# Scores of two heads issued together on the two halves of TensorE's rows, in two attentions of a two-block kernel

## The chip, the cores and the metric

The kernel runs on one core of a Trainium2 chip. The metric is the device time of one execution in microseconds; the median of three runs is given.

## What is computed

Two transformer blocks over 256 rows of width 1024, in float32. Only the parts with the two attentions that the change touches matter here:

```python
# first block: attention over keys chosen by an index score, 8 heads of 64
s = einsum(q, k) * 64 ** -0.5 - slopes[head] * distance     # masked keys -inf
out = softmax(s) @ v
# beside it: a causal depthwise convolution of 31 taps over 512 channels
# second block: banded attention, 8 heads of 64, with a relative bias per head
sc = einsum(qb, kb) * 64 ** -0.5 + rel_bias[head, clip(distance)]
ob = softmax(sc) @ vb
# and differential attention, 4 heads with two components of 64 each
attn = softmax(q0 k0) - lam * softmax(q1 k1);  oa = attn @ va
```

The second block goes on with a gated merge, a cross attention over 256 memory rows and a feed-forward layer.

## The kernel before

All engines run programs written out by hand, ordered by semaphores; there is no scheduler. Weights come as blocks of 1 MB on SP's queue. ScalarE rounds each half block (a "piece" of 1024 columns) to `w_hi` (L1232), VectorE makes the rest `w_lo` (L1696), in a ring of four slots, and TensorE multiplies a piece in 12 matmuls of 512 columns (L564 to L566). Ten pieces of the first block are "native": eight matmuls (L597) on unsplit weights, and neither ScalarE nor VectorE works for them.

`attention` on TensorE serves the first attention (tag `a1_`) and the banded one (`b_`). `STEPS` (L365) lists 16 steps (h, t): head h, row block t of 128 rows, with 128 keys for t = 0 and 256 for t = 1. Step n on TensorE is: transposes of the probabilities (`turn_p`, L804, one for t = 0 and two for t = 1, into bank 6), the scores of step n + 2 (L795) into bank 4 or 5, one piece of a projection for later (`between`), and the values of step n - 1 (L811, two records for t = 0, four for t = 1). A score has 64 rows, one head's width: even heads lie on rows 0 to 63, odd ones on 64 to 127. Each matmul of float32 scores or values leaves two records in the trace.

For step n VectorE adds the bias tile `bias_t` to the scores and takes the reduction in the same instruction (L2035 in the first attention, L1846 in the banded one); ScalarE takes the exponential (L1320), rounds a piece's weights, and copies the turned probabilities to `pT` (L1406). In the first attention the bias tile is made for every step (L2013) and VectorE also works off the convolution's taps (L1914), up to nine a step (`A1_TAPS`). In the banded one the tile is made once for each head (L1840). Scores of steps 0 and 1 are issued ahead of the loop, behind them one piece, and ahead of that VectorE and ScalarE already do their part of these steps (`project_slabs`).

In the banded attention TensorE also transposes the rotated keys of the differential attention, behind the piece of steps 1 and 2 (`TURN_AT`), four at a time into bank 7 (L1072), and ScalarE copies them to `kaT` (L1290). Behind the banded attention the differential one starts: its `d_scores` (L1088) issues the scores of a head's two components one behind the other, on the two row halves, into banks 4, 5 and 7 in turn (`D_BANKS`); its transposes are at L1098, its values at L1105.

## Time and profile before

| | |
|---|---|
| median of 3 runs | 954.34 us (953.24 to 954.71) |
| span of the profiled execution | 953.0 us |
| TensorE busy | 918.4 us, 96% of the span |
| VectorE busy | 627.9 us, 66% |
| ScalarE busy | 458.5 us, 48% |
| first attention | about 126 to 199 us |
| banded attention | about 519 to 586 us |

The time of the profiled execution itself is not listed apart from its span, which is 1.3 us below the median of the runs: that is what lies around a span. Ends of matmuls are modelled, so the distance between starts says more than a duration. A share of busy time is a mean over stages with different limits.

### The profile page before, as it was taken

What the parts mean: (1) busy time and instruction counts of PE and PEld (TensorE: products, weight loads), DVE (VectorE), ACT (ScalarE), POOL (GpSimd) and SP (SyncE); (2) the same over time, 40 slices, a digit from 0 to 9 for tenths busy, and PEclk for the clock granted to TensorE, in tenths of its full rate; (3) what the DMA queues carried; (4) which work ended last, traced back from release to release, by engine and by line L of the source; (5) the groups of instructions that cost most, each with busy time, mean ns of one, the idle gap of its engine ahead of it and who ended that gap; (6) DMA issues with size and microseconds to landing.
All of it is one profiled execution on the core that took longest, in us unless ns stands there. A gap on an engine that the chain in (4) does not pass through costs nothing.

```text
span 953.0 us, 11982 instructions
## 1 busy us (share of the span) xinstructions
PE 918.4 (96%) x4235; PEld 735.6 (77%) x4235; DVE 627.9 (66%) x1022; ACT 458.5 (48%) x709; POOL 31.7 (3%) x42
## 2 busy tenths in 40 slices
PE   4999999999999999999999999999999999999997
PEld 3877755688788888887887777788888788888785
DVE  4898999988755555676748445678656565555444
ACT  0554523465544444443654554674545465555442
POOL 2110000010000000000000000000000000000000
PEclk9999999999999999999999999999999999999999
DMA  9999324656485565575555343455451475655531
GB/s 331 353 386 352 114 79 145 232 204 219 134 265 180 190 192 187 195 263 171 189 190 184 91 152 112 133 177 199 149 204 46 133 221 183 190 193 182 177 133 44
DMA packets 103030, 178.10 MB, mean 187 GB/s; under 512 B 6318, under 2 KB 52635, under 8 KB 102986
## 3 DMA queue, kind: packets, MB, share of 16 engines
q1 hardware_dynamic: 96138, 151.23, 48.2%
q0 software_dynamic: 6848, 26.28, 7.5%
q8 instruction: 27, 0.44, 0.2%
q14 instruction: 17, 0.14, 0.0%
HBM read 176.39 MB, written 1.05 MB: 186 GB/s over the span
## 4 chain that ended last, share of the span: by engine, by line
PE 74%; DVE 12%; issue 7%; DMA 3%; ACT 2%; SPq 0%; POOL 0%; DVEq 0%; POOLq 0%; ACTq 0%
PE bank L564 18%; PE bank L566 18%; PE bank L565 18%; PE bank L976 10%; DVE conv_out L1914 5%; DVE w_lo L1696 2%; DMA tap_rows<-in_w_dw 1%; DMA raw_weights<-in_w_in 1%; ACT w_hi L1232 1%; PE bank L955 1%; DVE ada_acc L1772 1%; PE bank L643 1%; DMA ada_raw<-in_w_ada 1%; PE bank L795 1%; PE bank L635 1%
## 5 line engine op out<-in xcount | busy, mean ns | idle before, releaser
L1696 DVE TENSOR_TENSOR w_lo<-raw_weights,w_hi 128x1024 fp32r<-128x1024 f32 x267 | 324.2, 1223 | 229.2 <-ACT w_hi L1232 227.8
L1232 ACT ACTIVATE w_hi<-raw_weights 128x1024 fp32r<-128x1024 f32 x267 | 281.0, 1059 | 282.1 <-PE bank L566 200.3
L564 PE MATMUL bank<-w_hi,a_hi 128*128 128x512 f32 x808 | 323.5, 400 | 3.1 <-issue 1.3
L566 PE MATMUL bank<-w_hi,a_lo 128*128 128x512 f32 x808 | 315.9, 391 | 0.0
L565 PE MATMUL bank<-w_lo,a_hi 128*128 128x512 f32 x808 | 315.6, 391 | 0.0
L564 PEld LDWEIGHTS bank<-w_hi,a_hi 128*128 128x128 f32 x808 | 152.1, 188 | 40.6 <-issue 8.5
L566 PEld LDWEIGHTS bank<-w_hi,a_lo 128*128 128x128 f32 x808 | 152.1, 188 | 32.7
L565 PEld LDWEIGHTS bank<-w_lo,a_hi 128*128 128x128 f32 x808 | 152.4, 189 | 29.7 <-issue 0.2
L976 PE MATMUL bank<-w_hi,ff_hi 128*128 128x512 f32 x176 | 55.1, 394 | 0.8 <-DVE hidden_rows L2194 0.5
L976 PE MATMUL bank<-w_lo,ff_hi 128*128 128x512 f32 x176 | 54.2, 389 | 0.0
L976 PE MATMUL bank<-w_hi,ff_lo 128*128 128x512 f32 x176 | 54.2, 389 | 0.0
L1914 DVE SCALAR_TENSOR_TENSOR conv_out<-conv_in,conv_taps_T,conv_out 128x256 f32<-128x256 f32 x120 | 51.4, 489 | 0.0
L1320 ACT ACTIVATE probabilities<-masked_scores,row_stats 128x128 f32<-128x128 f32 (+1 forms) x32 | 14.6, 455 | 58.6 <-DVE row_stats L2035 41.4
L976 PEld LDWEIGHTS bank<-w_hi,ff_hi 128*128 128x128 f32 x176 | 32.7, 188 | 8.6 <-DVE hidden_rows L2194 0.9
L976 PEld LDWEIGHTS bank<-w_hi,ff_lo 128*128 128x128 f32 x176 | 33.0, 188 | 6.9
L976 PEld LDWEIGHTS bank<-w_lo,ff_hi 128*128 128x128 f32 x176 | 33.0, 188 | 6.9
L597 PE MATMUL bank<-raw_weights,feature_rows_early 128*128 128x512 f32 x80 | 36.7, 604 | 0.0
L597 PEld LDWEIGHTS bank<-raw_weights,feature_rows_early 128*128 128x128 f32 x80 | 14.5, 189 | 17.0 <-issue 16.5
L1772 DVE SCALAR_TENSOR_TENSOR ada_acc<-ada_start,row_stats,ada_acc 128x512 f32<-128x512 f32 x35 | 26.3, 751 | 1.1
L564 PE MATMUL bank<-w_hi,mem_hi 128*128 128x512 f32 x64 | 25.9, 404 | 0.0
L566 PE MATMUL bank<-w_hi,mem_lo 128*128 128x512 f32 x64 | 25.0, 391 | 0.0
L565 PE MATMUL bank<-w_lo,mem_hi 128*128 128x512 f32 x64 | 25.0, 390 | 0.0
(264 smaller groups left out, 860.2 us busy)
## 6 DMA issues: line engine op xcount, KB each, us to landing
raw_weights<-in_w_in SPq DMA_DIRECT2D x40, 1024.0 KB, 5.1
raw_weights<-in_w_ffn_in SPq DMA_DIRECT2D x44, 512.0 KB, 4.6
raw_weights<-in_w_gate_up SPq DMA_DIRECT2D x44, 512.0 KB, 4.6
ada_start<-in_w_ada POOLq DMA_DIRECT2D x11, 1024.0 KB, 10.8
raw_weights<-in_w_ffn_out SPq DMA_DIRECT2D x9, 1024.0 KB, 4.9
raw_weights<-in_w_down SPq DMA_DIRECT2D x9, 1024.0 KB, 4.9
ada_raw<-in_w_ada POOLq DMA_DIRECT2D x8, 1024.0 KB, 8.3
raw_weights<-in_w_out SPq DMA_DIRECT2D x8, 1024.0 KB, 5.1
```

The source lines that it names most:

```text
L564: pe.matmul(ps, hi[:, kt, ts], wh, start=start, stop=False)
L565: pe.matmul(ps, hi[:, kt, ts], wl, start=False, stop=False)
L566: return pe.matmul(ps, lo[:, kt, ts], wh, start=False, stop=stop)
L597: last = pe.matmul(ps, f_h1[:, kt, t * P:(t + 1) * P], w, start=(kt == 0), stop=(kt == 2 * n - 1))
L635: pe.matmul(bank[b][:, 0:SEQ], ident, const[:, 0:SEQ], start=True, stop=True)
L643: last = pe.transpose(bank[b0 + g][:, kk * SEQ + t * P:kk * SEQ + (t + 1) * P], src[:, t, c:c + P], ident)
L976: o = pe.matmul(bank[out_bank(t, c)][:], lhs[:, kt, ts], w[:, c * W:(c + 1) * W], start=(kt == 0 and n == 0), stop=(kt == KF - 1 and n == 2))
L1232: act.activation(w_hi[:, slot, 0:m], raw[:, b % RAW, half * PIECE:half * PIECE + m], ACT.Copy)\
L1320: act.activation(p_work[:, n % 2, 0, 0:keys], s_work[:, n % 2, 0, 0:keys], ACT.Exp, scale=-1.0, bias=stat[:, 32 + n % 2:33 + n % 2], accum ...
L1696: dve.tensor_tensor(w_lo[:, slot, 0:m], raw[:, b % RAW, half * PIECE:half * PIECE + m], w_hi[:, slot, 0:m], ALU.subtract).then_inc(lo_read ...
L1772: o = dve.scalar_tensor_tensor(out=slot, in0=w, scalar=c, in1=slot, op0=ALU.mult, op1=ALU.add)
L1914: dve.scalar_tensor_tensor(out=conv_out[:, g, :], in0=conv_in[:, g, k:k + SEQ], scalar=taps[:, g, k:k + 1], in1=conv_out[:, g, :], op0=ALU ...
```

## The change

It touches `attention` and what stands around it. `STEPS` is put in the order (h0, t0), (h1, t0), (h0, t1), (h1, t1), and so on by pairs of heads. Even steps issue the scores of steps n + 2 and n + 3 one behind the other, on the two row halves, odd steps issue none. The scores go to banks 4, 5 and 7 in turn, and wait for the reduction of step n - 3 where they waited for n - 2. The bias tile is doubled, and its making waits for one reduction less. As bank 7 is taken, the key transposes move to the second half of bank 6: two at a time, in steps 1 to 4, ahead of the step's own transposes, and ScalarE copies each two right behind `pT`.

```diff
--- before.py
+++ after.py
@@ -140,7 +140,7 @@
 FILL2 = (1,) * 24
 AHEAD2 = (0,) * 2 + (1,) * 22
 ROPE = (((0, 0), (0, 1)), ((0, 2), (1, 0)), ((1, 1), (1, 2)))
-TURN_AT = (1, 2)
+TURN_AT = (1, 2, 3, 4)
 LOOP_PIECES = sum(FILL2)
 AHEAD_PIECES = 4 + sum(AHEAD2)
 A1_TAPS = (1,) + (9,) * 10 + (7,)
@@ -238,13 +238,13 @@
     qxT = sb("qxT", [P, KD, SEQ], at=u_at)
     qx_rows = sb("qx_rows", [P, TT, D], at=u_at + 8192)
 
-    w_at = region(13 * 1024)
+    w_at = region(14 * 1024)
     ada_acc = sb("ada_acc", [P, 6, W], at=w_at)
     score = sb("score", [P, TT, SEQ], at=z_at + TT * IN1 * 4)
     s_work = sb("masked_scores", [P, 2, 2, SEQ], at=w_at + 2048)
     p_work = sb("probabilities", [P, 2, 2, SEQ], at=w_at + 6144)
     pT = sb("probabilities_T", [P, 2, TT, P], at=w_at + 10240)
-    bias_t = sb("bias_tile", [P, SEQ], at=w_at + 12288)
+    bias_t = sb("bias_tile", [P, 2, SEQ], at=w_at + 12288)
     relu_t = sb("relu_tile", [P, 2, SEQ], at=w_at + 6144)
     ada_late = [sb(f"ada_late{t}", [P, BLK], at=z_at + (t * IN1 + C_GA) * 4) for t in range(TT)]
     conv_hi = sb("conv_hi", [P, CG, SEQ], F32R, at=z_at + C_QI * 4)
@@ -362,7 +362,12 @@
 
         return 8 * slab - sum(pe_tiles(n) for n in range(min(2 * slab, 8)))
 
-    STEPS = [(h, t) for h in range(HEADS) for t in range(TT)]
+    STEPS = [(2 * pair + e, t) for pair in range(HEADS // 2) for t in range(TT) for e in range(2)]
+    SCORE_BANKS = (4, 5, 7)
+
+    def score_bank(n):
+
+        return bank[SCORE_BANKS[n % len(SCORE_BANKS)]]
 
     block = nc.Block()
     ctx = ExitStack()
@@ -783,16 +788,16 @@
                     pe.wait_ge(sem["q_moved"], 2)
                     turn4(6, C_K, z, sem["k_turned"])
 
-        def attention(tag, q, k, v_cols, pv_banks, between, first):
+        def attention(tag, q, k, v_cols, pv_banks, between, first, beside=lambda n: None):
 
 
             def scores(n):
                 h, t = STEPS[n]
                 keys = P * (t + 1)
                 half = slice(64 * (h % 2), 64 * (h % 2) + 64)
-                if n >= 2:
-                    pe.wait_ge(*after(tag, "max", n - 1))
-                pe.matmul(bank[4 + n % 2][:, 0:keys], q[half, h // 2, t * P:(t + 1) * P], k[half, h // 2, 0:keys],
+                if n >= 3:
+                    pe.wait_ge(*after(tag, "max", n - 2))
+                pe.matmul(score_bank(n)[:, 0:keys], q[half, h // 2, t * P:(t + 1) * P], k[half, h // 2, 0:keys],
                           start=True, stop=True).then_inc(event(tag, "scores"), 1)
 
             def turn_p(n):
@@ -800,6 +805,7 @@
                 pe.wait_ge(*after(tag, "exp", n + 1))
                 if n >= 1:
                     pe.wait_ge(*after(tag, "pT", n))
+                beside(n)
                 for kt in range(t + 1):
                     last = pe.transpose(bank[6][:, kt * P:(kt + 1) * P], p_work[:, n % 2, 0, kt * P:(kt + 1) * P], ident)
                 last.then_inc(event(tag, "turned"), 1)
@@ -816,8 +822,9 @@
             first(scores)
             for n in range(len(STEPS)):
                 turn_p(n)
-                if n + 2 < len(STEPS):
+                if n % 2 == 0 and n + 2 < len(STEPS):
                     scores(n + 2)
+                    scores(n + 3)
                 between(n)
                 if n >= 1:
                     values(n - 1)
@@ -1051,6 +1058,7 @@
             scores(1)
             piece(P_IN2 + 19, U_IN2 + 4, 3, 4)
             pe.wait_ge(sem["t2_copied_act"], 3)
+            pe.wait_ge(sem["t2_copied_dve"], 3)
 
         def mixed_piece(j):
 
@@ -1062,17 +1070,20 @@
 
             for j in range(filled(n, FILL2), filled(n + 1, FILL2)):
                 mixed_piece(j)
+
+        def turn_keys(n):
+
+            if n - 1 in TURN_AT:
+                pe.wait_ge(sem["t2_copied_act"], 4 + TURN_AT.index(n - 1))
             if n in TURN_AT:
                 g = TURN_AT.index(n)
                 pe.wait_ge(sem["rope_sum"], 2 * TT)
-                pe.wait_ge(*((sem["t2_copied_act"], 4) if g else (sem["t2_copied_dve"], 3)))
-                for kk in range(2):
-                    c = E_KA + (2 * g + kk) * P
-                    for t in range(TT):
-                        last = pe.transpose(bank[7][:, kk * SEQ + t * P:kk * SEQ + (t + 1) * P], z[:, t, c:c + P], ident)
+                for t in range(TT):
+                    last = pe.transpose(bank[6][:, SEQ + t * P:SEQ + (t + 1) * P],
+                                        z[:, t, E_KA + g * P:E_KA + (g + 1) * P], ident)
                 last.then_inc(sem["t2"], 1)
 
-        attention("b_", qbT, kbT, E_VB, 0, mixed_step, last_input_piece)
+        attention("b_", qbT, kbT, E_VB, 0, mixed_step, last_input_piece, turn_keys)
 
 
         DS = [(h, t) for h in range(4) for t in range(TT)]
@@ -1108,7 +1119,7 @@
 
         pe.wait_ge(*after("b_", "max", 16))
         pe.wait_ge(*after("b_", "pT", 16))
-        pe.wait_ge(sem["t2_copied_act"], 5)
+        pe.wait_ge(sem["t2_copied_act"], 7)
         d_scores(0)
         mixed_step(16)
         d_scores(1)
@@ -1391,7 +1402,7 @@
                     both(sem["k_turned"], kT, 6, sem["k_moved"])
             slab_out(P_IN1 + 4 * s + 3, U_IN1 + s, IN1_COLS[s], ACT.Sigmoid if s == 1 else ACT.Copy)
 
-        def softmax_steps(tag, between, weights, started):
+        def softmax_steps(tag, between, weights, started, beside=lambda n: None):
 
             for n in range(started, 1):
                 softmax_exp(tag, n)
@@ -1405,6 +1416,7 @@
                     act.wait_ge(*after(tag, "pv", n - 1))
                 act.activation(pT[:, n % 2, 0:t + 1, :], bank[6][:, 0:P * (t + 1)].rearrange("p (k n) -> p k n", k=t + 1),
                                ACT.Copy).then_inc(event(tag, "pT"), 1)
+                beside(n)
 
         def gate_out(n):
 
@@ -1543,9 +1555,6 @@
             for j in range(filled(n - 1, FILL2), filled(n, FILL2)):
                 if j % 4 == 3:
                     mixed_slab_out(j // 4)
-            if n - 1 in TURN_AT:
-                g = TURN_AT.index(n - 1)
-                copy_pair(sem["t2"], 7 + g, kaT[:, 2 * g:2 * g + 2, :], 7, sem["t2_copied_act"])
 
         def mixed_slab_out(m):
 
@@ -1565,7 +1574,14 @@
 
             conv(P_IN2 + 24 + filled(n, AHEAD2), AHEAD2[n])
 
-        softmax_steps("b_", mixed_out, mixed_weights, 2)
+        def keys_out(n):
+
+            if n in TURN_AT:
+                g = TURN_AT.index(n)
+                act.wait_ge(sem["t2"], 7 + g)
+                act.activation(kaT[:, g, :], bank[6][:, SEQ:2 * SEQ], ACT.Copy).then_inc(sem["t2_copied_act"], 1)
+
+        softmax_steps("b_", mixed_out, mixed_weights, 2, keys_out)
 
         def d_exp(n):
             keys = P * (n % 2 + 1)
@@ -1835,15 +1851,15 @@
             if n == 0:
                 dve.wait_ge(sem["rel_landed"], 16)
             if t == 0:
-                if n:
-                    dve.wait_ge(*after("b_", "max", n))
-                dve.scalar_tensor_tensor(out=bias_t[:], in0=rel_rows[:, h, ::-1], scalar=8.0, in1=C("chunk"),
+                if n >= 2:
+                    dve.wait_ge(*after("b_", "max", n - 1))
+                dve.scalar_tensor_tensor(out=bias_t[:, h % 2, :], in0=rel_rows[:, h, ::-1], scalar=8.0, in1=C("chunk"),
                                          op0=ALU.mult, op1=ALU.add).then_inc(event("b_", "bias"), 1)
                 dve.wait_ge(*after("b_", "bias", h + 1))
             dve.wait_ge(*after("b_", "scores", n + 1))
             if n >= 2:
                 dve.wait_ge(*after("b_", "exp", n - 1))
-            dve.tensor_tensor_reduce(s_work[:, n % 2, 0, 0:keys], bank[4 + n % 2][:, 0:keys], bias_t[:, SEQ - keys:],
+            dve.tensor_tensor_reduce(s_work[:, n % 2, 0, 0:keys], score_bank(n)[:, 0:keys], bias_t[:, h % 2, SEQ - keys:],
                                      -DH ** -0.5, 3e38, ALU.add, ALU.min, stat[:, 32 + n % 2:33 + n % 2])\
                 .then_inc(event("b_", "max"), 1)
 
@@ -2008,9 +2024,9 @@
 
             h, t = STEPS[n]
             keys = P * (t + 1)
-            if n:
-                dve.wait_ge(*after("a1_", "max", n))
-            dve.scalar_tensor_tensor(out=bias_t[:, 0:keys], in0=C("rel", SEQ - keys), scalar=2.0 ** -(h + 1),
+            if n >= 2:
+                dve.wait_ge(*after("a1_", "max", n - 1))
+            dve.scalar_tensor_tensor(out=bias_t[:, n % 2, 0:keys], in0=C("rel", SEQ - keys), scalar=2.0 ** -(h + 1),
                                      in1=score[:, t, 0:keys], op0=ALU.mult, op1=ALU.add).then_inc(event("a1_", "bias"), 1)
 
         late_done = [0]
@@ -2032,7 +2048,7 @@
             dve.wait_ge(*after("a1_", "bias", n + 1))
             if n >= 2:
                 dve.wait_ge(*after("a1_", "exp", n - 1))
-            dve.tensor_tensor_reduce(s_work[:, n % 2, 0, 0:keys], bank[4 + n % 2][:, 0:keys], bias_t[:, 0:keys],
+            dve.tensor_tensor_reduce(s_work[:, n % 2, 0, 0:keys], score_bank(n)[:, 0:keys], bias_t[:, n % 2, 0:keys],
                                      -DH ** -0.5, 3e38, ALU.add, ALU.min, stat[:, 32 + n % 2:33 + n % 2])\
                 .then_inc(event("a1_", "max"), 1)
             here = A1_TAPS[n] if n < len(A1_TAPS) else 0
```

## Rows read from the trace of the kernel before

**Rows 1.** The page, chain that ended last, shares of the span

```profile
PE 74%; DVE 12%; issue 7%; DMA 3%; ACT 2%; SPq 0%; POOL 0%; DVEq 0%; POOLq 0%; ACTq 0%
```

**Rows 2.** Groups of TensorE's instructions: busy us, mean ns, idle before

```profile
L795 PE MATMUL bank<-kbT,qbT 64*128 64x128 f32 (+1 forms) x32 | 9.2, 372 | 0.0
...
L1088 PE MATMUL bank<-kaT,qaT 64*128 64x128 f32 (+1 forms) x32 | 5.1, 375 | 0.0
```

**Rows 3.** Windows: length, busy us (count) of PE, PEld, DVE, ACT, POOL; clock, DMA, GB/s

```profile
120.00:184.00 64.00, 62.37 (x215) 35.45 (x214) 63.06 (x179) 19.61 (x50) 0.75 (x1) 1.00 0.44 150
...
543.00:551.00 8.00, 8.00 (x40) 6.23 (x39) 4.03 (x10) 4.16 (x11) 0.00 (x0) 1.00 0.42 133
597.00:598.00 1.00, 1.00 (x4) 0.81 (x4) 1.00 (x4) 0.00 (x0) 0.00 (x0) 0.50 0.07 16
```

**Rows 4.** TensorE's timeline, end of the banded attention: start, duration, line, count

```profile
570.75 0.33 PE L811 MATMUL bank<-z_projected,probabilities_T 128*128 128x64 f32 x2
570.92 0.28 PE L804 MATMUL bank<-constants,probabilities 128*128 128x128 f32 x1
...
574.79 0.39 PE L804 MATMUL bank<-constants,probabilities 128*128 128x128 f32 x2
...
578.76 0.28 PE L804 MATMUL bank<-constants,probabilities 128*128 128x128 f32 x1
...
582.03 0.39 PE L804 MATMUL bank<-constants,probabilities 128*128 128x128 f32 x2
...
585.02 0.78 PE L811 MATMUL bank<-z_projected,probabilities_T 128*128 128x64 f32 x6
```

**Rows 5.** TensorE's timeline, differential attention

```profile
589.98 0.83 PE L1088 MATMUL bank<-kaT,qaT 64*128 64x128 f32 x4
...
609.60 0.27 PE L1098 MATMUL bank<-constants,probabilities 128*128 128x128 f32 x1
609.79 0.49 PE L1088 MATMUL bank<-kaT,qaT 64*128 64x128 f32 x4
...
613.54 0.38 PE L1098 MATMUL bank<-constants,probabilities 128*128 128x128 f32 x2
...
617.55 0.27 PE L1098 MATMUL bank<-constants,probabilities 128*128 128x128 f32 x1
```

**Rows 6.** TensorE's timeline, start of the banded attention

```profile
519.18 0.92 PE L795 MATMUL bank<-kbT,qbT 64*128 64x128 f32 x4
...
523.30 0.30 PE L804 MATMUL bank<-constants,probabilities 128*128 128x128 f32 x1 [0.25 <-ACT probabilities L1320]
```

**Rows 7.** Timeline of all engines, middle of the banded attention

```profile
545.02 0.36 ACT L1406 ACTIVATE probabilities_T<-bank 128x256 f32<-128x256 f32 x1
...
547.39 0.28 PE L804 MATMUL bank<-constants,probabilities 128*128 128x128 f32 x1
```

**Rows 8.** Timeline of all engines, first attention

```profile
173.31 0.31 DVE L2035 CUSTOM_DVE_ANT_0 masked_scores<-bank,bias_tile 128x128 f32<-128x128 f32 x1
...
178.56 0.44 DVE L2035 CUSTOM_DVE_ANT_0 masked_scores<-bank,bias_tile 128x256 f32<-128x256 f32 x1
...
180.90 0.30 PE L804 MATMUL bank<-constants,probabilities 128*128 128x128 f32 x1 [1.30 <-ACT probabilities_T L1406]
```

**Rows 9.** Timeline of all engines, end of the first attention

```profile
197.07 1.05 ACT L1232 ACTIVATE w_hi<-raw_weights 128x1024 fp32r<-128x1024 f32 x1
...
197.43 0.75 DVE L1772 SCALAR_TENSOR_TENSOR ada_acc<-ada_start,row_stats,ada_acc 128x512 f32<-128x512 f32 x1
...
198.15 1.22 DVE L1696 TENSOR_TENSOR w_lo<-raw_weights,w_hi 128x1024 fp32r<-128x1024 f32 x1
```

**Rows 10.** TensorE's timeline, second turn of the differential attention

```profile
595.62 0.44 PE L1098 MATMUL bank<-constants,probabilities 128*128 128x128 f32 x2 [1.84 <-DVE probabilities L2307]
...
596.86 0.71 PE L564 MATMUL bank<-w_hi,a_hi 128*128 128x512 f32 x1
...
600.35 0.40 PE L566 MATMUL bank<-w_hi,a_lo 128*128 128x512 f32 x1
```

## The prediction

> **What bounds the kernel now.** I read the page first, for the chain of work that ended last: matmuls hold 74% of it, VectorE 12% [rows 1]. So a microsecond of TensorE time is worth a microsecond in most stretches, and the question is in which of the two attentions this one is. The table of windows answers it [rows 3]. In the banded attention (543 to 551 us) TensorE is busy 8.00 of 8.00 us, VectorE 4.03 and ScalarE 4.16: TensorE alone sets the pace. In the first attention (120 to 184 us) TensorE is busy 62.37 of 64 us, but VectorE 63.06 of 64: it works through the convolution's taps beside the attention without a pause. Both look full, and there the waits must say who waits for whom.
>
> They do. In the second half of the first attention VectorE takes 5.25 us from one step's scores to the next (173.31 to 178.56), and TensorE then stands idle 1.30 us until ScalarE has copied the last turned probabilities; its transpose starts 2.34 us after VectorE began on that step's scores [rows 8]. TensorE waits for VectorE, through ScalarE.
>
> **What a group of scores costs TensorE.** The time from one step's transposes to the next's is one step. From 570.92 to 578.76 are two steps, one with a 128-key and one with a 256-key score: 7.84 us [rows 4]. The next step has no score and takes 3.27 us (578.76 to 582.03). The one behind it has none either: 2.99 us to its first values, and 0.17 us for values of two records (570.75 to 570.92), so 3.16 us [rows 4]. Two steps without scores are 6.43 us, and the two scores cost 1.41. Alone, the 128-key one costs (574.79 - 570.92) - 3.27 = 0.60 us, which leaves 0.81 for the 256-key one.
>
> What does a pair on the two row halves cost? The differential attention already issues such pairs (L1088), each from one head's two components into two of the banks 4, 5 and 7. Two steps of it, one with a 128-key pair and one with a 256-key pair, take 7.95 us (609.60 to 617.55) [rows 5]. The two banded steps with one score each take 7.84 [rows 4], and are otherwise alike but for values half as wide. So a pair costs what one score costs, or at most (7.95 - 7.84) / 2 = 0.05 us more. The grouped lines agree: 32 records of mean 375 ns cover only 5.1 us as pairs, and 9.2 us as singles of the same mean, 372 ns [rows 2]. I take the pair at the price of one, 0.60 and 0.81 us.
>
> **The change part by part.** *Pairs in the banded attention.* Before, steps 0 to 13 each issue one score, seven of each length: 7 x 1.41 = 9.87 us. After, the even steps issue a pair and the odd ones nothing: 256-key pairs at steps 0, 4, 8 and 12, 128-key ones at 2, 6 and 10, so 4 x 0.81 + 3 x 0.60 = 5.04 us. That is 4.83 us less on the engine that sets the pace. The two scores issued ahead of the loop cover 0.92 us now [rows 6] and would cover the 0.49 of a 128-key pair [rows 5]. That gain is worth nothing: the first transpose at 523.30 already waits 0.25 us for the first exponential [rows 6], which hangs on VectorE's work and not on these scores. The wait becomes about 0.7 us.
>
> *Waits of the pair.* Scores n+2 need step n-1's bank read, scores n+3 step n's. Both reads lie before exponential n, for which the transposes of step n have waited already. So neither wait costs anything. Bound from the other side: the one pair of the differential attention whose second half had to wait covers 0.83 us where a free one covers 0.49 [rows 5], or 0.34 more; seven times that is 2.4 us.
>
> *Does anything else become late?* The nearest chain in the banded attention is ScalarE's copy of the turned probabilities: the one at 545.02 takes 0.36 us, and TensorE's next transposes are at 547.39 [rows 7], 2.0 us later. The steps shrink by 0.35 us on average, and an odd step by at most 0.81, so more than 1 us is left.
>
> *Key transposes moved.* The eight transposes of the rotated keys go from two groups into bank 7, behind a piece, to four groups of two into the free half of bank 6, before the step's own transposes. The number is the same: nothing for TensorE. ScalarE's two copies of 512 columns become four of 256, behind the copy of the probabilities: about 0.3 us more before each of four waits, inside the 2.0 us above. Without that cover it would be 4 x 0.3 = 1.2 us. Banks 4 and 5 get no transposes; no DMA and no place in SP's or POOL's queues changes, and a block of weights is asked for when its piece is used, so earlier.
>
> *Two bias tiles.* VectorE's tile operations stay the same in number and size; only their wait gets looser by one step. Before the banded loop two 256-wide tiles are made instead of one (about 0.35 us), the second behind the first score's reduction, so the first exponential keeps its time. Zero.
>
> *Pairs in the first attention.* TensorE saves the same 4.83 us, but until 183 us VectorE sets the time and its work is not touched: TensorE only waits longer. From step 12 on TensorE has no long waits. There it issues one 256-key pair instead of a 128- and a 256-key score, 0.60 us less. This moves ScalarE's last weight copy (197.07) up by 0.60, but VectorE's subtraction behind it begins at 198.15, straight after a product that began at 197.43 and takes 0.75 us [rows 9]. So nothing is won. The Trainium skill (TensorEngine Tiling (Array Packing), PSUM Bottleneck) warns that tiling speeds up TensorE but not the evacuation of PSUM. By that warning alone both attentions would gain nothing; the windows say that it holds in the first and not in the second.
>
> Sum: 4.8 us. The profiled execution spans 953.0 us, and with it 948.2. The median of the runs shown is 954.34, 1.3 us above that span; I carry the 1.3 along: 949.5 us.
>
> **The rivals.**
> *A clock fall in the first attention.* TensorE's waits grow there. A step without scores is 3.2 us and VectorE's is 5.25, so the wait ahead of step 10 is 5.25 - 3.2 = about 2.0 us, longer than any now in that stretch. Behind an idle time of 1.84 us [rows 10] the granted clock was 0.50 [rows 3], the 1.2 GHz level, and eight matmuls took 3.49 us (596.86 to 600.35) [rows 10], 0.44 each. A step without scores at the 2.4 GHz level, 3.27 us with its 12 matmuls [rows 4], leaves them 0.25 at the most. So a fall costs about 1.6 us. One such fall before 183 us disappears into VectorE's time. One behind step 12 costs 1.6 less the 0.6 us that TensorE gains there unused: 1.0 us, so 950.5. Against it: 1.30 us of idle at 180.90 [rows 8] brought no fall.
> The Trainium skill (TensorE: Matmul & The Clock Gate, What's actually happening) calls the throttled clock the default which activity releases; by it emptier steps make this likelier, and 950.5 would be the time. The rows show one fall and one idle time without any.
>
> *The clock stays down.* This one ends on the other side. If the longer waits keep TensorE at 1.2 GHz from step 9 to the end of the attention, the last three pieces take 12 x 0.2 = 2.4 us more each. The transposes, scores and values of steps 12 to 15, about 0.5 us a step, double as well: 2 us. That is 9.2 us less 0.6, against a gain of 4.8: 3.8 us slower, 958.1. It turns into a loss once the slow stretch behind step 12 costs 5.4 us, or about 27 slow matmuls. For it: the waits repeat each step. Against it: the fall seen here lasted 3.5 us, and behind step 12 the waits are short.
>
> *The halves don't overlap*, because a wait stands between the two matmuls: 2.4 us less gain, 951.9. Most pairs at L1088 have such a wait too and overlap, so this is unlikely.
>
> *The first attention gains as well*, if TensorE and not VectorE sets its end: another 4.8 us, 944.7 us. Against it: VectorE's 63.06 of 64 us.
>
> **How the numbers follow.** Forecast 0.57 (own range 948.9 to 950.2); one clock fall 0.16; no overlap 0.09; first attention too 0.04; clock stays down 0.06; a small unforeseen wait that eats most of the gain (952.5 to 956) 0.08. The range 948.0 to 952.2 holds the first three, 0.82: its low end takes in a pair that costs some 0.2 us less than one score, its high end the pair with a wait at the full 0.34 us. A measurement of this kernel can tell about 0.2%, 1.9 us, from no change. Faster by more are the first four, 0.86; within it the unforeseen wait, 0.08; slower the stuck clock, 0.06.
>
> **What the changed profile would show.** In the banded attention L795's 32 records should cover about 5 us, not 9.2, and the time from first transposes to the differential attention's first scores (523.30 to about 585.7, some 62.4 us) should shrink to 57.6 us, with TensorE still without idle time. In the first attention VectorE should reach step 12 at 183.4 us as now, with more idle time on TensorE before that. The prediction is wrong if banded steps begin to wait for ScalarE's key copies, if the clock is below 1.00 behind 184 us, or if L795's pairs cover 0.8 us and more.

## The result and the profile after

The changed kernel takes 949.99 us (median of 5 runs, 948.37 to 950.44), and the kernel before, run beside it, 954.71 us (median of 5, 953.24 to 955.35). The ratio is 0.9942, with a 95% interval from 0.9927 to 0.9957, so the change takes off some 0.6%. The forecast was 949.5 us, its range 948.0 to 952.2. The profiled execution took 949.03 us and spans 947.2 us, against a span of 953.0 before. In every run on record the time is 1.7 to 1.9 us above its span.

I cut both profiled executions at the same six places of TensorE's timeline: the first scores of the first attention, the transposes behind its output, the first scores and the first transposes of the banded attention, the first scores of the differential attention, and the transposes behind its output. In us:

| stretch | before | after | difference |
|---|---|---|---|
| up to the first scores | 125.72 | 126.39 | +0.67 |
| first attention | 75.20 | 75.12 | -0.08 |
| to the banded attention's first scores | 318.26 | 318.22 | -0.04 |
| those scores to its first transposes | 4.12 | 4.11 | -0.01 |
| banded loop | 62.43 | 57.61 | -4.82 |
| differential attention | 36.54 | 34.97 | -1.57 |
| the rest | 330.73 | 330.78 | +0.05 |

Two rows matter: the banded loop, on which the forecast rested, and the differential attention, of which it said nothing. The later start of 0.67 us belongs to this execution: it lies before anything that the change touches, and in a later profile of the same kernel the first scores come at 125.60 us. Over the 13 profiled executions of this study they come between 125.60 and 128.49 us, so an execution's start alone moves its time by up to 2.9 us.

The page's chain of the changed kernel, shares of the span by engine:

```profile
PE 72%; DVE 13%; issue 8%; DMA 4%; ACT 2%; SPq 0%; POOL 0%; DVEq 0%; POOLq 0%; ACTq 0%
```

TensorE holds 72% of it against 74% [rows 1]. The groups of TensorE's instructions of the changed kernel (busy us, mean ns of one, idle time before):

```profile
L1099 PE MATMUL bank<-kaT,qaT 64*128 64x128 f32 (+1 forms) x32 | 5.1, 375 | 0.0
...
L800 PE MATMUL bank<-kbT,qbT 64*128 64x128 f32 (+1 forms) x32 | 4.8, 375 | 0.0
```

The mean of the 32 banded scores stays (375 ns, 372 before), but they cover 4.8 us where they covered 9.2 [rows 2]: records that lie on top of each other count once. Now they lie as close as the differential ones. The windows of the changed kernel (length, then busy us and count of PE, PEld, DVE, ACT and POOL, then granted clock, DMA share and GB/s):

```profile
120.00:184.00 64.00, 60.69 (x215) 34.84 (x214) 63.08 (x179) 19.02 (x49) 0.75 (x1) 0.97 0.43 152
543.00:551.00 8.00, 8.00 (x43) 6.46 (x42) 4.38 (x8) 4.22 (x10) 0.00 (x0) 1.00 0.41 134
176.00:180.00 4.00, 3.81 (x13) 2.97 (x14) 4.00 (x11) 0.33 (x2) 0.00 (x0) 0.61 1.02 383
592.00:600.00 8.00, 8.00 (x43) 6.06 (x43) 5.92 (x19) 4.49 (x13) 0.00 (x0) 1.00 0.42 133
```

From 543 to 551 us TensorE is still busy 8.00 of 8.00 us, now with 43 records in place of 40, and VectorE and ScalarE have come up only to 4.38 and 4.22 us [rows 3]: TensorE still sets the pace of the banded attention. From 120 to 184 us TensorE's busy time fell from 62.37 to 60.69 us, and VectorE's 63.06 stayed as it was, at 63.08. The first attention is VectorE's, as before. TensorE's timeline of the changed kernel, at the start and at the end of the banded attention:

```profile
519.73 0.49 PE L800 MATMUL bank<-kbT,qbT 64*128 64x128 f32 x4
...
523.84 0.30 PE L810 MATMUL bank<-constants,probabilities 128*128 128x128 f32 x1 [0.68 <-ACT probabilities L1331]
524.07 0.70 PE L800 MATMUL bank<-kbT,qbT 64*128 64x256 f32 x4
```

```profile
581.45 0.49 PE L1099 MATMUL bank<-kaT,qaT 64*128 64x128 f32 x4
```

The pair issued ahead covers 0.49 us where the two singles covered 0.92, and the wait of the first transpose grew from 0.25 to 0.68 us [rows 6]: the gain went into that wait. From there to the differential scores it is 581.45 - 523.84 = 57.61 us.

TensorE's timeline in the first attention of the changed kernel, around its longest wait:

```profile
176.19 0.41 PE L810 MATMUL bank<-constants,probabilities 128*128 128x128 f32 x2 [2.25 <-ACT probabilities_T L1417]
176.53 0.49 PE L800 MATMUL bank<-kT,qT 64*128 64x128 f32 x4
176.95 0.79 PE L569 MATMUL bank<-w_hi,a_hi 128*128 128x512 f32 x1
177.54 0.63 PE L570 MATMUL bank<-w_lo,a_hi 128*128 128x512 f32 x1
...
179.68 0.63 PE L569 MATMUL bank<-w_hi,a_hi 128*128 128x512 f32 x1
180.10 0.49 PE L570 MATMUL bank<-w_lo,a_hi 128*128 128x512 f32 x1
180.43 0.39 PE L571 MATMUL bank<-w_hi,a_lo 128*128 128x512 f32 x1
```

VectorE's scores of steps 10 and 11 in the same stretch:

```profile
173.87 0.42 DVE L2051 CUSTOM_DVE_ANT_0 masked_scores<-bank,bias_tile 128x256 f32<-128x256 f32 x1
...
179.25 0.43 DVE L2051 CUSTOM_DVE_ANT_0 masked_scores<-bank,bias_tile 128x256 f32<-128x256 f32 x1
```

VectorE still takes 5.38 us from one step's scores to the next, and TensorE, with one group of scores less to do, waits 2.25 us at 176.19. Behind that wait the granted clock averages 0.61 from 176 to 180 us, so most of that window lies at the 1.2 GHz level, and matmuls of 0.39 us are stretched to 0.63. It costs nothing: the matmuls are back at 0.39 by 180.43, and VectorE's next scores at 179.25 came on its own time, with none of TensorE's work late for them. The stretch as a whole takes 75.12 us, and it takes 75.12 us as well in a later kernel with the same first attention whose clock did not fall there (the one with the other order in the differential attention, below).

At its end TensorE waits for VectorE once more:

```profile
201.51 1.09 PE L648 MATMUL bank<-constants,z_projected 128*128 128x128 f32 x8 [0.58 <-DVE z_projected L2078]
```

TensorE had come to these transposes some 0.6 us sooner than before, and the 0.6 us go into this wait.

### The profile page after: what moved, and what is told of

It is laid out like the page before. It is cut to its first block, busy times and chain, and to the rows that moved or that the text cites. A ratio compares the mean times of both kernels' runs of the same rounds, so it can differ in the third digit from the quotient of the medians.

```text
span 947.2 us, 11986 instructions
## 1 busy us (share of the span) xinstructions
PE 908.8 (96%) x4235; PEld 730.6 (77%) x4235; DVE 627.1 (66%) x1022; ACT 457.7 (48%) x711; POOL 31.7 (3%) x42
## 4 chain that ended last, share of the span: by engine, by line
PE 72%; DVE 13%; issue 8%; DMA 4%; ACT 2%; SPq 0%; POOL 0%; DVEq 0%; POOLq 0%; ACTq 0%
PE bank L569 18%; PE bank L571 17%; PE bank L570 17%; PE bank L983 10%; DVE conv_out L1930 5%; DVE w_lo L1712 2%; ACT w_hi L1243 1%; DVE ada_acc L1788 1%; DMA raw_weights<-in_w_in 1%; DMA tap_rows<-in_w_dw 1%; PE bank L962 1%; PE bank L648 1%; DMA ada_raw<-in_w_ada 1%; PE bank L640 1%; PE bank L1186 1%
```

## The experiments

### Each attention alone, and pairs taken apart

The first four kernels keep everything of the changed kernel (banks, bias tiles, moved key transposes) and choose for each of the two attentions in which order its steps go and whether two scores are issued together. The edit, here with the values of the first kernel:

```diff
+    BY_HEAD = [(h, t) for h in range(HEADS) for t in range(TT)]
+    BY_PAIR = [(2 * pair + e, t) for pair in range(HEADS // 2) for t in range(TT) for e in range(2)]
+    STEPS_OF = {"a1_": BY_HEAD, "b_": BY_PAIR}
+    GROUPED = {"a1_": False, "b_": True}
...
-                if n % 2 == 0 and n + 2 < len(STEPS):
-                    scores(n + 2)
-                    scores(n + 3)
+                if n + 2 < len(STEPS_OF[tag]) and (n % 2 == 0 or not GROUPED[tag]):
+                    scores(n + 2)
+                    if GROUPED[tag]:
+                        scores(n + 3)
```

**Pairs in the banded attention alone.**

> Pairs in the banded attention only; the first attention goes back to steps head by head and one score a step (still three banks and two bias tiles). Theory (only the banded loop gains, the first attention's time is VectorE's): the loop from its first transposes to the differential attention's first scores 57.6 us as in the changed kernel, the whole 4.7 to 4.8 us faster than the kernel before, no different from the changed kernel. Rival (the first attention carries part of the gain, hidden by a late start in the profiled execution): 2.4 us or less faster.

Measured: 949.67 us (median of 6, 948.79 to 951.97), before 955.28; ratio 0.9948 (0.9935 to 0.996). The banded loop takes 57.61 us, just as in the changed kernel, so this half of the edit carries all of the gain. The first attention took 76.56 us in the profiled execution, 1.4 more than in the kernel before, and VectorE's timeline says why:

```profile
196.33 0.75 DVE L1792 SCALAR_TENSOR_TENSOR ada_acc<-ada_start,row_stats,ada_acc 128x512 f32<-128x512 f32 x1
198.34 0.57 DVE L1789 TENSOR_SCALAR ada_acc<-ada_start,row_stats 128x512 f32<-128x512 f32 x1 [1.27 <-DMA ada_start<-in_w_ada]
```

VectorE stood idle 1.27 us until a DMA had brought a block of weights. The kernel with two scores of one head together, below, has the same order of steps and shows 1.17 us of it, while the kernel before, also by heads, shows none; whether the order has a part in it stays open. The interval, as time saved, reaches from 3.8 to 6.2 us. It holds the expected 4.7 to 4.8, and not quite the 3.5 that would be left if these 1.3 us stood in every execution. The profiled one, 951.55 us, is 1.9 above the median.

**Pairs in the first attention alone.**

> Pairs in the first attention only; the banded one goes back to steps head by head and one score a step, with its key transposes where the change put them. Theory: banded loop 62.4 us, the whole within 0.5 us of the kernel before, TensorE idle ahead of the late steps of the first attention up to about 2 us. Rival: 2.4 us or more faster.

Measured: 954.54 us (11 runs); ratio 0.9994 (0.998 to 1.0008), no change that can be measured. The first attention takes 75.12 us and the banded loop 62.37. The wait before step 10 is there too (2.27 us at 175.84), with seven stretched matmuls from 176.6 to 179.33 us, and costs nothing here either. In the banded attention this kernel has the old order and single scores, but the third bank, the second bias tile and the moved key transposes: together they cost nothing (62.37 us, 62.43 before).

**Two scores together, but of one head, so that both lie on the same row half.**

```diff
+    STEPS_OF = {"a1_": BY_HEAD, "b_": BY_HEAD}
+    GROUPED = {"a1_": True, "b_": True}
```

> Both attentions issue scores by twos in even steps, but in the old order head by head, so that the two of a group lie on the same half of the rows and only one change between 64 and 128 rows is saved, no work overlaps. Theory (most of the gain is overlap, a smaller part the saved changes): a group costs 0.85 us (as the two ahead of the loop do from start to start) plus the 0.2 us that the next matmul loses, 1.05 against 1.41 for two single ones, so the banded loop 62.4 - 7 x 0.36 = 59.9 us and the whole about 2.5 us faster than before. Rival (the gain is all saved changes, the halves do not overlap): 57.6 and 4.8 us faster. Second rival (all is overlap): 62.4 and no gain.

Measured: 952.57 us (10 runs); ratio 0.9976 (0.9966 to 0.9986); banded loop 59.69 us. A group on one half, on TensorE's timeline, and then the 32 banded scores in the groups of instructions:

```profile
562.39 0.92 PE L803 MATMUL bank<-kbT,qbT 64*128 64x128 f32 x4
```

```profile
L803 PE MATMUL bank<-kbT,qbT 64*128 64x128 f32 (+1 forms) x32 | 7.4, 350 | 0.0
```

The four records follow one another for 0.92 us, where the pair on two halves covered 0.70 with 256 keys and 0.49 with 128. So the gain of 4.8 us has two parts. Seven groups where there were fourteen are worth 62.43 - 59.69 = 2.74 us, 0.39 each; laying the two scores on different halves gives another 59.69 - 57.61 = 2.08 us. With seven groups TensorE changes seven times less between scores and the full-height work around them; that this change is what costs the 0.39 us is the likely reading, but no run separates it from whatever else a second score right behind the first may save. The expectation had the loop nearly right (59.9 us) and the shares the wrong way round: it called the overlap most of the gain, and it is the smaller part.

**The new order of the steps, one score at a time.**

```diff
+    STEPS_OF = {"a1_": BY_PAIR, "b_": BY_PAIR}
+    GROUPED = {"a1_": False, "b_": False}
```

> The new order by pairs of heads, the three banks, the two bias tiles and the moved key transposes, but one score in each step. Theory (order, banks and tiles bring nothing by themselves): banded loop 62.4 us, the whole within 0.7 us of the kernel before. Rival (the third bank or the second bias tile takes waits away): more than 2 us faster.

Measured: 955.62 us (10 runs); ratio 1.0005 (0.9996 to 1.0014); banded loop 62.82 us. The groups of instructions:

```profile
L803 PE MATMUL bank<-kbT,qbT 64*128 64x128 f32 (+1 forms) x32 | 9.0, 375 | 0.0
```

The 32 scores cover 9.0 us again. So the order by pairs of heads, the third bank, the second bias tile and the moved transposes give nothing by themselves; issuing the two halves back to back does. The loop is even 0.4 us longer. As the kernel with the old order and the new banks took 62.37 us, this belongs to the order. Half of it can be counted: the two scores ahead of the loop are now both 128-key ones, which leaves eight 256-key scores in the loop where there were seven, and one costs 0.81 - 0.60 = 0.21 us more. The changed kernel has this order too and the kernel with groups on one half has not. So the 2.08 us of the halves are what is left after it, and the overlap alone may be worth up to 2.5.

### Is the first attention's gain hidden behind VectorE?

Both kernels here leave out 12 of the convolution's 31 taps, which takes work off VectorE in the first attention (their output is that of a shorter convolution):

```diff
+KEPT = 19
...
-A1_TAPS = (1,) + (9,) * 10 + (7,)
+A1_TAPS = (1,) + (5,) * 9 + (4,)
```

> The kernel before with 12 of the convolution's 31 taps left out (taps 19 to 30 are not added), so that VectorE has 48 of its 124 tap instructions less, all of them in the first attention's steps (up to 5 a step where there were 9, some 1.6 us less a step). The output is that of a shorter convolution. It is the base for the next kernel. VectorE's 5.25 us a step become about 3.6, less than TensorE's 3.9: TensorE then sets the time, and its 2.7 us of waits between 134 and 204 us should mostly go: about 2 us less than before.

> The changed kernel with the same 12 taps left out. Theory (the first attention's gain exists on TensorE and was hidden by VectorE's taps): with VectorE out of the way the pairs are worth 4 to 5 us there as well, so 8.5 to 9.5 us less than the same kernel before without these taps. Rival (the first attention cannot gain from pairs for another reason: ScalarE's copies, the native pieces): about 4.8 us less than it, as with all taps.

The kernel before with fewer taps measured 952.24 us (10 runs; ratio 0.9963, 0.995 to 0.9976), the changed one with fewer taps 942.22 us (4 runs; ratio 0.9856, 0.9838 to 0.9875). The windows from 120 to 184 us of the one and of the other:

```profile
120.00:184.00 64.00, 63.92 (x225) 36.84 (x224) 48.80 (x140) 22.77 (x56) 0.75 (x1) 1.00 0.43 151
```

```profile
120.00:184.00 64.00, 64.00 (x249) 38.34 (x248) 51.82 (x153) 24.08 (x59) 0.75 (x1) 1.00 0.48 164
```

With VectorE at 48.80 us, TensorE is busy 63.92 of 64 us and sets the time, and now the pairs pay in the first attention as well: it shrinks from 72.49 to 67.10 us, by 5.4 us, the banded loop shrinks by 4.83, and the whole by 10.0 us by the medians, a little more than the 8.5 to 9.5 expected. Of the 5.4 us, 0.4 lie in the two scores ahead of the loop, which this stretch takes in: from them to the next matmul it was 0.85 us, and is 0.42. In the full kernel the same edit was worth 0.08 us there. This is the clearest evidence of the study that the gain in the first attention is made and then swallowed by VectorE's work.

### The wait in the differential attention

In the changed kernel's differential attention TensorE waits 1.85 us, as before. The two timelines of the changed kernel, VectorE's and then TensorE's:

```profile
588.48 1.23 DVE L1712 TENSOR_TENSOR w_lo<-raw_weights,w_hi 128x1024 fp32r<-128x1024 f32 x1 [2.11 <-ACT w_hi L1243]
589.62 0.28 DVE L2306 CUSTOM_DVE_ANT_0 masked_scores<-bank,constants 128x128 f32<-128x128 f32 x1
...
590.82 0.48 DVE L2323 SCALAR_TENSOR_TENSOR probabilities<-probabilities,component_stats 128x256 f32<-128x256 f32 x1
```

```profile
589.12 0.39 PE L571 MATMUL bank<-w_hi,a_lo 128*128 128x512 f32 x1
591.36 0.44 PE L1109 MATMUL bank<-constants,probabilities 128*128 128x128 f32 x2 [1.85 <-DVE probabilities L2323]
...
592.60 0.47 PE L569 MATMUL bank<-w_hi,a_hi 128*128 128x512 f32 x1
```

VectorE waits 2.11 us for ScalarE's weight copy at 588.48, makes `w_lo` from it, and only behind that come the reductions of the next scores and the mixing (the two components of a head put together, L2323) that TensorE needs at 591.36; VectorE is done with it at 591.30. The edit lets the mixing of the second step go ahead of that subtraction (`mixed_weights` makes the `w_lo` of a piece):

```diff
-            mixed_weights(16 + n)
+            if n == 1:
+                mixed_weights(16)
+            if n:
+                mixed_weights(16 + n)
```

> The changed kernel, and in the differential attention VectorE mixes the second step's probabilities before it makes the weight residue of the first piece of that loop (one instruction of 1.2 us moved behind four short ones). Theory: the 1.85 us for which TensorE waits ahead of the second transposes go almost entirely, as VectorE sits there waiting for ScalarE's rounded piece while the exponentials are done; and with them goes the clock fall behind this wait where an execution has one (another 1.6 us): 1.5 to 3.4 us faster than the changed kernel, about 947.5. Rival (the wait moves to the residue, as its piece is needed next): no difference from the changed kernel.

> The changed kernel once more, as it is, beside the others on one chip. Its profiled execution spanned 5.8 us less than that of the kernel before, its runs 4.7 us. If this was one missing clock fall behind the wait of the differential attention (1.6 us), a matter of the execution and not of the change, then a fall should be seen there this time as in most other executions, the span should be near 949, and the median of the runs stay at 4.7 to 5.2 us below the kernel before. Rival (the change took the fall away): no fall here either.

The kernel with the other order measured 946.61 us (6 runs, 945.69 to 948.71; ratio 0.991, 0.9894 to 0.9927), and the changed kernel beside it 949.07 us (6 runs; ratio 0.9934, 0.9918 to 0.9951). So the order is worth 2.46 us by the medians, within the 1.5 to 3.4 expected. It is the best kernel of the study. VectorE's and TensorE's timelines with the other order:

```profile
586.13 0.29 DVE L2306 CUSTOM_DVE_ANT_0 masked_scores<-bank,constants 128x128 f32<-128x128 f32 x1 [0.23 <-PE bank L1099]
...
587.84 0.48 DVE L2323 SCALAR_TENSOR_TENSOR probabilities<-probabilities,component_stats 128x256 f32<-128x256 f32 x1
588.24 1.22 DVE L1712 TENSOR_TENSOR w_lo<-raw_weights,w_hi 128x1024 fp32r<-128x1024 f32 x1
```

```profile
588.90 0.38 PE L1109 MATMUL bank<-constants,probabilities 128*128 128x128 f32 x2
589.21 0.70 PE L1099 MATMUL bank<-kaT,qaT 64*128 64x256 f32 x4
```

The mixing ends at 588.32 us, 3.0 earlier, of which about 0.5 is this execution's own earlier start. TensorE has no wait there, and the differential attention takes 32.89 us instead of 34.97.

The second thing asked of the repeat was whether the clock falls behind the wait of 1.85 us. It had fallen in the kernel before and in each of the six experiments ahead of this one, with the same wait, but not in the changed kernel. The expectation was that it would fall this time, and that missed:

```profile
590.53 0.44 PE L1109 MATMUL bank<-constants,probabilities 128*128 128x128 f32 x2 [1.85 <-DVE probabilities L2323]
```

Nothing is stretched behind it, and the differential attention again takes 34.97 us. The gap of the medians, expected at 4.7 to 5.2 us, came out at 955.01 - 949.07 = 5.94.

### Bias tiles made by GpSimd

If VectorE's work sets the first attention, work taken off it should pay. The 16 bias tiles can go to GpSimd, which idles there (0.75 us busy in 64); it makes each with a multiplication and an addition:

```diff
-            dve.scalar_tensor_tensor(out=bias_t[:, n % 2, 0:keys], in0=C("rel", SEQ - keys), scalar=2.0 ** -(h + 1),
-                                     in1=score[:, t, 0:keys], op0=ALU.mult, op1=ALU.add).then_inc(event("a1_", "bias"), 1)
+            pool.tensor_scalar(bias_t[:, n % 2, 0:keys], C("rel", SEQ - keys), 2.0 ** -(h + 1), None, ALU.mult)\
+                .then_inc(sem["scaled_bias"], 1)
+            pool.wait_ge(sem["scaled_bias"], n + 1)
+            pool.tensor_tensor(bias_t[:, n % 2, 0:keys], bias_t[:, n % 2, 0:keys], score[:, t, 0:keys], ALU.add)\
+                .then_inc(event("a1_", "bias"), 1)
```

> [...] Theory (in the first attention VectorE's work sets the time until step 12, and TensorE's there is cover): VectorE loses 0.21 us (128 keys) or 0.34 us (256 keys) a tile from start to start, for the 12 steps up to 183 us about 3.3 us. Behind step 12 it waits 0.5 to 0.6 us a step for ScalarE's weight copies anyway, and nothing is won. The first attention shrinks from 75.1 to about 71.9 us, the banded loop stays at 57.6, and the median is about 946 us. Rival one (the tiles come late): the first three steps are 1.0 to 4 us apart, so a tile of GpSimd's that takes over 1 us makes VectorE wait at steps 1 and 2, some 1 to 2 us. Rival two (GpSimd slows VectorE down while both work): the products beside it take longer than 0.41 us each, and the gain is eaten, 949 us or more.

> As the one before, and with the two normalisation steps of the differential attention in the other order, which took 2.1 to 2.5 us off the changed kernel. Theory: the two are in different stretches and add up: about 2.3 us below the run with GpSimd's tiles alone, some 943.5 us. Rival: the fall of the clock in the differential attention is missing in some executions anyway, so that the order is worth only the wait of 1.85 us, 944.2 us.

The theory fell. GpSimd's tiles alone: 957.24 us (12 runs; ratio 1.0021, 1.0007 to 1.0036), first attention 83.15 us where 71.9 was expected and the changed kernel has 75.12. With the other order in the differential attention: 954.53 us (12 runs; ratio 0.999, 0.9978 to 1.0002), first attention 83.12 us. The difference of the two, 2.71 us, is once more what that order is worth. GpSimd's timeline of the first of them, and VectorE's:

```profile
133.97 0.84 POOL L545 TENSOR_SCALAR bias_tile<-constants 128x256 f32<-128x256 f32 x1
134.89 0.92 POOL L548 TENSOR_TENSOR bias_tile<-bias_tile,score 128x256 f32<-128x256 f32 x1
...
147.66 1.02 POOL L545 TENSOR_SCALAR bias_tile<-constants 128x256 f32<-128x256 f32 x1 [2.56 <-DVE row_stats L2062]
...
172.54 0.82 POOL L514 DMA_DIRECT2D ada_start<-in_w_ada  x1 [14.53 <-PE bank L623]
...
174.05 0.45 POOL L548 TENSOR_TENSOR bias_tile<-bias_tile,score 128x128 f32<-128x128 f32 x1
```

```profile
134.35 4.73 DVE L1951 SCALAR_TENSOR_TENSOR conv_out<-conv_in,conv_taps_T,conv_out 128x256 f32<-128x256 f32 x9
...
139.34 3.87 DVE L1951 SCALAR_TENSOR_TENSOR conv_out<-conv_in,conv_taps_T,conv_out 128x256 f32<-128x256 f32 x9
...
147.50 4.26 DVE L1951 SCALAR_TENSOR_TENSOR conv_out<-conv_in,conv_taps_T,conv_out 128x256 f32<-128x256 f32 x9
...
165.45 3.64 DVE L1951 SCALAR_TENSOR_TENSOR conv_out<-conv_in,conv_taps_T,conv_out 128x256 f32<-128x256 f32 x9
...
174.63 0.29 DVE L2062 CUSTOM_DVE_ANT_0 masked_scores<-bank,bias_tile 128x128 f32<-128x128 f32 x1 [4.40 <-issue]
```

Two costs show. Nine of VectorE's products take 3.64 us where GpSimd is idle (165.45), but 3.87 beside a tile of 128 keys (139.34) and 4.26 beside one of 256 (147.50), which GpSimd began at 147.66: a loss of 0.2 and 0.6 us for the 0.21 and 0.34 us saved. Beside two tiles it was 4.73 us (134.35). The Trainium skill (SBUF — State Buffer, SBUF: two separate sides) says that GpSimd and VectorE share a pair of ports under an exclusive lock, and that a VectorE instruction with two SBUF operands takes part in it when GpSimd's reads SBUF. The products have two such operands, and the rows agree. And before step 9 VectorE stood idle 4.40 us, because that tile was queued on GpSimd behind a DMA whose own wait ended at 172.54. The mend puts it ahead of the DMA:

```diff
-        for n in range(9):
+        for n in range(10):
             selected_bias(n)
         ada_block(17)
-        for n in range(9, 16):
+        for n in range(10, 16):
```

> As the run with GpSimd's tiles, but the tile of step 9 is made ahead of GpSimd's DMA of the weight block, whose own wait had held it until 172.5 us there, so that VectorE stood idle 4.4 us before step 9. Theory (two costs: the late tile, and GpSimd slowing VectorE while it works): VectorE's step 8 already came 2.0 us late in the run before, where no tile was late but the first two, because nine products took 3.87 to 4.26 us from start to start beside a tile and 3.64 without one. The mend takes away the 4.4 us and what followed from them alone: a first attention of 77.5 to 79 us, still 2 to 4 us over the 75.1 of the changed kernel, a median of 951 to 953 us. Rival (the late tile was all, the rest a start-up cost of 0.8 us): 75 us less, near 72.7, and a median near 947 us.

Measured: 955.12 us (10 runs, 952.8 to 957.11), before 955.76; ratio 0.9995 (0.998 to 1.001). Both expected values were missed: the median by 2 us (951 to 953), and the first attention took 80.04 us where 77.5 to 79 was expected: 3.1 us less than without the mend, and still 4.9 more than with VectorE's own tiles. GpSimd's timeline and VectorE's:

```profile
173.84 2.40 POOL L545 TENSOR_SCALAR bias_tile<-constants 128x256 f32<-128x256 f32 x1
176.33 0.72 POOL L548 TENSOR_TENSOR bias_tile<-bias_tile,score 128x256 f32<-128x256 f32 x1
```

```profile
177.18 0.42 DVE L2062 CUSTOM_DVE_ANT_0 masked_scores<-bank,bias_tile 128x256 f32<-128x256 f32 x1 [1.64 <-issue]
```

The expectation had left one tile out: now the tile of step 10 stands behind that DMA, its multiplication takes 2.40 us where the others of this size took 0.84 to 1.29, and VectorE waits 1.64 us for it. The rival, that the late tile was all, is off by over 7 us.

## Why the prediction held, point by point

**What a group of scores costs, and a pair at the price of one.** The step gave 9.87 us for 14 singles and 5.04 for seven pairs, a difference of 4.83. The loop shrank by 4.82 us, in the changed kernel and with the banded pairs alone. Whether the two terms are right one by one the loop doesn't say; the grouped lines (9.2 to 4.8 us) fit them. Where the 4.8 us come from the prediction did not say: it took the price of a pair as found, and that over half of it goes to having fewer groups only the kernel with groups on one half showed. That the sum came out to 0.01 us is in part luck. The new order costs single scores 0.4 us, of which the sum holds 0.21 (the eight 256-key scores); if the other 0.2 stand in the changed kernel too, a pair costs a little less than was put down.

**Scores ahead of the loop: hidden.** Right: 0.49 us, and a wait of 0.68 where about 0.7 was named.

**The pair's waits cost nothing.** Right. The bound of 2.4 us wasn't touched; a 128-key pair covers 0.49 us, as the free one did [rows 5].

**Nothing else becomes late in the banded attention.** Right: TensorE has no idle time in the loop behind its first transpose. Key transposes and bias tiles at zero: right, by the kernel with pairs in the first attention alone, whose banded loop has both and takes 62.37 us against 62.43.

**The first attention gains nothing.** Right (0.08 us), and for the reason given: with fewer taps the gain is there. VectorE reaches step 12 at 184.10 us, which is 183.43 without the later start, against 183.40 before. The wait before step 10 was put at about 2.0 us and measured 2.25, and the 0.6 us that TensorE was to gain unused behind step 12 stand as its wait of 0.58 us at 201.51. The Trainium skill (TensorEngine Tiling (Array Packing), PSUM Bottleneck) warns that row and column tiling doesn't speed up what empties PSUM. The traces agree for the first attention, where the engine that reads the scores was already full (for the most part with the convolution's products), and not for the banded one, which won 4.82 us.

**The rivals.** The clock fall in the first attention came, but before 183 us, where the prediction said it would disappear; it did, and from 184 us to the end of the attention the granted clock was 1.00. Of four profiled executions with that wait of 2.25 to 2.28 us three show a fall, and the mean clock of the stretch went from 1.00 to 0.97 [rows 3]. The Trainium skill (TensorE: Matmul & The Clock Gate, What's actually happening) calls the throttled clock the default that activity releases; the emptier steps bear that out in direction, in three executions of four. The clock didn't stay down, the halves do overlap (worth 2.08 us, where their absence was priced at 2.4), and the first attention gains only with the taps left out.

**What the prediction did not have.** The differential attention was 1.57 us shorter, since the granted clock stayed at 1.00 from 592 to 600 us behind the same wait after which it had been 0.50 before [rows 3, 10]. It is also why the profiled difference is 5.8 us where the sum gave 4.8; the later start took 0.67 back. The medians differ by 4.72 us, and by 5.94 in the repeat. Against the forecast of 949.5 us the median is 0.5 us high. The forecast carried over the 1.3 us between the span and the median of the kernel before as what lies around a span; that is 1.7 to 1.9 us in every run, and the rest is how the profiled execution lies among the others. In the changed kernel the span lies 2.8 us below the median, as the profiled execution was itself 1.0 us faster than it. So that the total came so close owes something to luck. All of this is within what the comparison can tell: its interval, as time saved, reaches from 4.1 to 7.0 us.

**Left open.** What decides whether the clock falls behind the wait of 1.85 us. With the same instructions in the differential attention it fell in the kernel before, in six experiments and in the mended GpSimd kernel, and did not in the changed kernel, its repeat and the first GpSimd kernel. It is not the edit that takes the fall away, for the kernel before lacks it in some executions too, as the mean clock of a whole run tells. The one profiled execution without any fall in these stretches has 0.999, those with one or two have 0.995 to 0.997. Of the 82 runs of the kernel before that the four comparisons list, ten have 0.999 and spans of 951.2 to 953.2 us (median 951.4), the other 72 have 0.994 to 0.998 and a median of 954.0. That is more than the 1.6 us of one fall, so something else, such as the start, goes into it as well. The spans of the repeat's six runs lie at 946.3 to 946.5 and at 948.0, 948.1 and 949.3 us; a gap of some 1.6 us would fit a fall in the differential attention, but a mean clock doesn't say in which attention a fall stood, and no trace of the longer ones exists. This last reading is argued, not shown. Open too is how much of the 4.72 and 5.94 us between the medians such falls make up.

## What to carry to other kernels

Where TensorE has no idle time and no other engine is near full, issue 64-row matmuls of different row halves back to back: here a little under half of the gain was the overlap, the rest came with having half as many groups of scores between the full-height work, whichever half they lie on. Before that, read which engine the stretch belongs to: the same edit was worth 4.8 us in one attention, 0.1 in the other, and 5.4 there once VectorE had less to do. Moving elementwise work to an idle GpSimd can cost VectorE more than it takes off: here the first attention grew by 4.9 to 8.0 us. It is worth looking first for an instruction that waits for a late operand and stands ahead of work that the pace-setting engine needs: moving one such instruction took 2.5 us off.

## What the runs showed of the hardware

An idle time of TensorE of 1.8 to 2.3 us is followed by the 1.2 GHz level in some executions and not in others: behind the wait of 1.83 to 1.85 us in the differential attention in 8 profiled executions of 11, behind that of 2.25 to 2.28 us in the first attention in 3 of 4. Waits of 1.30 to 1.78 us in the first attention were followed by none, in seven cases, and those of 3.65 and 4.34 us in the GpSimd kernels by one in all three. With the other order in the differential attention the same wait stood in the first attention:

```profile
175.77 0.41 PE L810 MATMUL bank<-constants,probabilities 128*128 128x128 f32 x2 [2.28 <-ACT probabilities_T L1417]
```

After these 2.28 us no matmul was stretched, where 2.25 us in the changed kernel were followed by seven at 0.63 us or more (176.95 to 179.68).

GpSimd's work slows VectorE's: the nine products above took 3.64 us alone and 3.87 to 4.73 us beside tiles, up to 30% longer. One multiplication of GpSimd's of 128 x 256 took between 0.84 and 2.40 us; that VectorE stretches it is likely, but no run has GpSimd alone to compare.
